# Residual rows kept in device memory during the expert stage, the eighth expert's gate and up weights in their place

## The reference, cut to what matters

```
x = x + gate_m * hybrid_mixer(h, ...)          # residual rows, 512 x 1024
h = rmsnorm(x, norm_ffn) * (1 + scale_f) + shift_f
# hierarchical_moe: each token goes to 2 of 32 experts
for e in range(32):
    hid = silu(tok @ w_gate[e]) * (tok @ w_up[e])
    out = out + combine[:, e:e+1] * (hid @ w_down[e])
x = x + gate_f * out
return rmsnorm(x, norm_final)
```

## Time and profile before

| | us |
|---|---|
| median of 3 runs | 1348.65 |
| lowest and highest of them | 1348.15, 1349.63 |
| the profiled execution, its own time | 1349.31 |
| span of its trace | 1347.4 |

### The profile page before, as it was taken

How to read it: one execution, slowest core, us unless ns; L and a number is a source line. 1 busy time by engine, 2 the same in 40 slices (tenths; PEclk the granted TensorE clock), 3 DMA queues, 4 the chain that set the end, 5 groups by cost and what they waited for, 6 DMA issues and landing times.

```text
span 1347.4 us, 17637 instructions
## 1 busy us (share of the span) xinstructions
PE 1279.5 (95%) x7322; PEld 983.3 (73%) x7322; DVE 648.6 (48%) x789; ACT 385.8 (29%) x504; POOL 277.8 (21%) x258
## 2 busy tenths in 40 slices
PE   6999999999999999999999999999989969979986
PEld 5888878877878888888887888777877845534443
DVE  3322633356466365474576722227772446434434
ACT  4222445543242132231325432223322300000003
POOL 1420000003022031130212000173343023323313
PEclk9999999999999999999998999999999979989989
DMA  6522332443425446254351223224005989999996
GB/s 248 195 94 93 110 134 102 146 182 124 158 72 214 152 172 234 93 208 166 125 199 65 91 94 98 90 94 142 2 33 166 365 308 416 417 417 416 418 419 252
DMA packets 45426, 253.41 MB, mean 188 GB/s; under 512 B 9056, under 2 KB 9712, under 8 KB 18220
## 3 DMA queue, kind: packets, MB, share of 16 engines
q1 hardware_dynamic: 36380, 227.99, 44.8%
q0 software_dynamic: 7024, 17.07, 3.4%
q10 hardware_dynamic: 1952, 7.34, 1.4%
HBM read 240.57 MB, written 20.99 MB: 194 GB/s over the span
## 4 chain that ended last, share of the span: by engine, by line
PE 83%; DMA 5%; DVE 5%; issue 3%; ACT 2%; POOL 1%; SPq 1%; POOLq 0%; DVEq 0%; ACTq 0%
PE ps L361 22%; PE ps L363 21%; PE ps L362 21%; PE ps L2358 6%; PE ps L2376 3%; DMA experts<-in_w_exp 2%; PE ps L2193 1%; PE ps L2346 1%; DVE experts L1356 1%; DMA arena<-h,arena 1%; SPq L613 1%; DMA y<-arena 1%; DMA arena<-y 1%; PE ps L1902 1%; DMA ident<-in_ident 0%
## 5 line engine op out<-in xcount | busy, mean ns | idle before, releaser
L346 DVE TENSOR_TENSOR w_low<-raw,w_high 128x2048 fp32r<-128x2048 f32 x81 | 214.4, 2647 | 263.1 <-ACT w_high L342 263.1
L361 PE MATMUL ps<-u_high,w_high 128*128 128x512 f32 (+1 forms) x712 | 279.2, 392 | 1.5 <-DVE u_low L329 1.5
L363 PE MATMUL ps<-u_high,w_low 128*128 128x512 f32 (+1 forms) x712 | 277.4, 390 | 0.0
L362 PE MATMUL ps<-u_low,w_high 128*128 128x512 f32 (+1 forms) x712 | 277.4, 390 | 0.0
L342 ACT ACTIVATE w_high<-raw 128x2048 fp32r<-128x2048 f32 x81 | 154.8, 1911 | 161.1 <-PE ps L363 132.6
L361 PEld LDWEIGHTS ps<-u_high,w_high 128*128 128x128 f32 (+1 forms) x712 | 133.0, 187 | 32.1 <-issue 3.6
L363 PEld LDWEIGHTS ps<-u_high,w_low 128*128 128x128 f32 (+1 forms) x712 | 133.0, 187 | 28.8
L362 PEld LDWEIGHTS ps<-u_low,w_high 128*128 128x128 f32 (+1 forms) x712 | 133.0, 187 | 28.2 <-issue 0.2
L361 PE MATMUL ps<-w_high,v_high 128*128 128x512 f32 x320 | 125.4, 392 | 2.8 <-POOL v_low L1740 2.8
L363 PE MATMUL ps<-w_high,v_low 128*128 128x512 f32 x320 | 124.7, 390 | 0.0
L362 PE MATMUL ps<-w_low,v_high 128*128 128x512 f32 x320 | 124.6, 390 | 0.0
(11 more groups left out here) (403 smaller groups left out, 1724.5 us busy)
## 6 DMA issues: line engine op xcount, KB each, us to landing
raw<-in_w SPq DMA_DIRECT2D x82, 1024.0 KB, 5.0
experts<-in_w_exp SPq DMA_DIRECT2D x69, 1024.0 KB, 22.3
arena<-in_w_exp SPq DMA_DIRECT2D x30, 1024.0 KB, 20.4
arena<-in_w_ada SPq DMA_DIRECT2D x24, 1024.0 KB, 4.9
y<-experts ACTq DMA_DIRECT2D x4, 1024.0 KB, 4.8
gates<-arena POOLq DMA_DIRECT2D x16, 256.0 KB, 2.3
arena<-gates POOLq DMA_DIRECT2D x2, 2048.0 KB, 9.5
arena<-y SPq DMA_DIRECT2D x4, 1024.0 KB, 7.8
```

What stands on the lines that cost most here:

```text
L346: dve.tensor_tensor(WL[:, 1 - s, :], RAW[:, 1 - s, :], WH[:, 1 - s, :].bitcast(F32), ALU.subtract).then_inc(lo_ready, 1)
L361: pe.matmul(out, a[0], b[0], start=start, stop=False)
L362: pe.matmul(out, a[0], b[1], start=False, stop=False)
L363: return pe.matmul(out, a[1], b[0], start=False, stop=stop)
```

## The change

The four chunks of `X` are sent to a new tensor `x_mid` in device memory as soon as they are complete. Gate and up of expert 7 (`RING`) then go into the place of `X`, under the name `NEXT`, and `gate_up(7)` reads them there. Behind the last expert's weights SP brings `X` back, and GpSimd waits for that ahead of the final sums. All these transfers count on the semaphore `gm_in` (`x_moves`).

```diff
+        NEXT = X[:, :, :].rearrange("p c n -> p (c n)")
...
+        x_moves, x_base = gm_in, 16
...
-                if b >= RING and before is not None:
+                if b > RING and before is not None:
                     sp.wait_ge(unit_done, M0 + before + 1)
-                for part in range(2):
+                for part in range(2 * (b != RING)):
                     w = slice(UNIT * part, UNIT * part + UNIT)
                     sp.dma_start(SLOTS[slot][:, w], e[:, w]).then_inc(gu_in[slot], 16)
                 if b >= RING and before is not None:
...
             expert_part(4, 0, gu_in)
+            for c in range(NC - 1):
+                sp.wait_ge(wo2_add, 5 + c)
+                sp.dma_start(t["x_mid"][P * c:P * c + P, :], X[:, c, :]).then_inc(x_moves, 16)
             sp.wait_ge(unit_done, M0)
             expert_part(2, 1, gu_in)
+            sp.wait_ge(wo2_add, 4 + NC)
+            sp.dma_start(t["x_mid"][P * (NC - 1):S, :], X[:, NC - 1, :]).then_inc(x_moves, 16)
             expert_part(3, 0, gu_in)
...
             expert_part(5, 0, gu_in)
+            sp.wait_ge(x_moves, x_base + 16 * NC)
+            sp.wait_ge(xr_tr, NC)
+            for part in range(2):
+                w = slice(UNIT * part, UNIT * part + UNIT)
+                sp.dma_start(NEXT[:, w], t["w_exp"][RING, :, w]).then_inc(x_moves, 16)
             for b in range(RING, OVER_AT):
                 expert_weights(b)
...
             for b in range(OVER_AT, N_EXP):
                 expert_weights(b)
+            for c in range(NC):
+                sp.dma_start(X[:, c, :], t["x_mid"][P * c:P * c + P, :]).then_inc(x_moves, 16)
             sp.wait_ge(over_y, 16 * n + 16)
...
             for c in range(NC):
+                pool.wait_ge(x_moves, x_base + 32 * NC + 32)
                 pool.wait_ge(chunk_in[c], 32)
                 pool.tensor_tensor(X[:, c, :], X[:, c, :], YC[:, c, 0, :], ALU.add).then_inc(chunk_in[c], 1)
...
-                pe.wait_ge(gu_in[slot], count)
+                if b == RING:
+                    pe.wait_ge(x_moves, x_base + 16 * NC + 32)
+                else:
+                    pe.wait_ge(gu_in[slot], count - 32 * (slot == 0 and b > RING))
+                weights = NEXT if b == RING else SLOTS[slot]
...
+    aps["x_mid"] = nc.dram_tensor("x_mid", [S, D], F32, kind="Internal").ap()
```

More of the change, by code:

```diff
@@ L2358, in gate_up @@
                         last = pe.matmul(PS[BLOCK * g:BLOCK * g + BLOCK, bank, 0:256], XT[:, x, P * c + BLOCK * h:P * c + BLOCK * h + BLOCK],
-                                         SLOTS[slot][:, HALF * k + 256 * g:HALF * k + 256 * g + 256], start=k == 0, stop=k == KD - 1)
+                                         weights[:, HALF * k + 256 * g:HALF * k + 256 * g + 256], start=k == 0, stop=k == KD - 1)
                 last.then_inc(unit_done, 1)
```

## The result

The changed kernel takes 1356.69 us (median of 5 runs, 1353.85 to 1358.93), the kernel before beside it 1349.07 us (5 runs): a ratio of 1.0057 [1.0046, 1.0068], some 7.6 us slower. The direction was forecast; the size was not. 1351.7 us stood on record, with 1354.4 us as its upper end. The profiled execution of the changed kernel took 1356.69 us itself, span 1354.6 us against 1347.4 us.

The account below looks back on a forecast made before the run. The expert stage was taken as a weight stream, its end set by the unbroken stream's start and bytes, with a tail behind. 0 + 0.6 + 2.5 = 3.1 us on 1348.65 gave 1351.7 us, range 1349.0 to 1354.4.

Parts of the forecast that it names:

- Part 1: Expert 7's gate and up sent early, ahead of the unbroken weight stream: 0 us, at most winning the hole, some 2 us.
- Part 2: Four stores of X beside those of `h2`: 1.4 us spill, delaying two weight parts and the gather's landing; 0.6 us taken.
- Part 3: Read-back of X behind the last weights delays the releasing scatter and `y`: 2.5 us, bounds 0 and 5.1.
- the scatter's: The scatter releasing the `y` loads shares engines with the read-back: 0 to 5.1 us late, 2.1 us taken.
- the other way: At the `y` loads, the slowest engine ends read-back and scatter at 1327.6, so its share of `y` is 2.6 us late.
- The rival in which everything collides: Scatter pays in full, 4.2 to 5.1 us, and the 1.4 us spill hits the first gather: 1354.7 us; chance 0.15.

## Why the prediction was too low, step by step

**Part 1, the early weights: 0. Right, and for the reason given.** Alone they measured 1.0006 [0.9995, 1.0016], and the down part of expert 7 still waits for the first down product. One premise was too narrow, that the end follows from when the unbroken stream starts: with the gather first the first down product ended 0.7 us sooner than before and the hole was gone, and the front was no shorter. What had gone through by then counts as well. The Trainium skill (DMA: Bandwidth & Descriptors, section Rules for kernel authors) advises to issue early and wait late; the reason it gives is that the fixed setup cost overlaps. The parts sent at 1094.99, 15 us ahead of the down part, won nothing: engines that were full gave an early transfer nothing.

**Part 2, the stores: 0.6 us with bounds 0 and 1.4. This step failed; it measured 3.8 in the change's profile and 2.8 in that without read-back.** The spill itself was sized well: from 1081 to 1084 the engines moved 257 GB/s instead of 63, which is 0.58 MB, or 1.4 us at 417 GB/s, as worked out. What failed is the sentence that `h2` is then out 1.4 us later and the gather still leaves at 1085.48. The last store landed 3.4 us later, since it is there only when the last of its engines is done, and two of them were late: the trace has a completion for each of the 16, all but two of them were in by 1083.77, and the last two came at 1084.68 and 1085.61. From 1070 to 1090 (half-microsecond digits) before and after:

```profile
DMA  8699968988999979999984200092799899899870
```

```profile
DMA  9799965999788999999999999411000009089999
```

The mean share is down to 4 at 1082.5 and at 1 or less from 1083.0 to 1086.0, yet the store's landing came at 1085.61. `h2` became the gather's releaser (+1.0 us), its two waiting weight parts left with the gather instead of ahead of it (another 2.8 us), and in the meantime SP had nothing to send. The working priced bytes; the cost was an order that turned, and engines that stood. The prediction had used just this spread among engines in its third part, but not here.

**Part 3, the read-back: 2.5 us with bounds 0 and 5.1. Sized within its bounds, 3.4.** Of its two ways only the scatter's was real (3.35 us, 2.1 expected). The better size stood in the other way: it has the last engine through with the read-back and the scatter's share at 1327.6, which is 3.7 us behind the scatter's old landing at 1323.94, but it used that for `y` alone and priced the scatter at half of 6.6 - 2.4. The way through the engines' order at the loads of `y` did not occur: the loads go out after the scatter, when the read-back is through, and the first of them landed 4.8 us after its issue. Missed was that a late `y` leaves TensorE standing, and that its clock may then fall for a while: 2.4 us between the medians without early weights; with the gather first the difference of 1.1 us is not clear of the noise, and in the change's own profile the clock stayed at 1.00.

By the Trainium skill's rule that each engine takes its queues in turn (DMA: Bandwidth & Descriptors, section Queues, rings and completion order) the prediction put the scatter's delay at 1.3 us, an estimate for an engine of mean load. The trace shows 3.35, set by the engines that were still busy when the others were through. The same section also says that a completion signal lands only after every earlier write of its engine, across its queues. No run here tests that: the scatter's data was late itself, by 5.04 - 1.97 = 3.07 us at its last packet.

**The sum.** 0 + 3.8 + 3.4 = 7.2 us in the traces (7.16 from front and tail together), 7.6 by the medians, against a forecast of 3.1: 3.2 us of what it lacked are Part 2 and 0.9 us Part 3. The rival in which everything collides had the mechanism at both ends and 1354.7 us; it put 1.4 us on the front.

## What to carry to other kernels

When the DMA engines carry an unbroken stream to the end, count how long they stand before it, or the bytes that have gone through by then: moving a transfer earlier wins only if it goes through where they stood. A small transfer that others wait for landed here with what was queued beside it, so before new bytes are put into a gap, look for the small landing in the same microseconds and ask what will leave SP together with it. What paid here was to give SP something to send at the hole itself: gate and up ahead of a down part that waits, 1345.98 us, faster than either kernel.

## What the runs showed of the hardware that was not expected

The small landing behind a drain: the same scatter took 2.4 to 3.0 us without a read-back beside it, 4.72 beside half the read-back, 5.8 to 5.9 beside all of it, in every profile.

The clock after a wait: in the five profiles with a full read-back and no zeroing TensorE stood for 3.15 to 3.45 us, and in three of them the granted clock fell below 1.00 behind that (0.50 after 3.41 us), in two it stayed at 1.00 (after 3.30 and 3.35 us). In the kernel with gather and gate and up first, 2.28 us of standing came ahead of a gate and up that took 5.36 us where it is 3.67 elsewhere, at a granted clock of 0.64 from 1322 to 1326:

```profile
1321.16 5.36 PE L2363 MATMUL ps<-experts,arena 128*64 128x256 f32 x32 [2.28 <-DMA experts<-in_w_exp]
```
